# Scores with 64 features: two heads, or two maps, matmul by matmul in turn on the two row halves of TensorE's array

## The chip, the cores and the metric

The kernel runs on one core of one Trainium2 chip. The metric is the device time of one execution in microseconds. Three runs of the kernel before are given, with their median.

## The reference, cut to what matters

Two transformer blocks stand one behind the other, on 512 tokens of 1024 features, in float32. Two of their attention mixers have scores over 64 features, and these are what is changed.

The first block's second mixer is a dilated band attention with 12 heads of 64 features, in three groups of four heads with dilations 1, 4 and 16. Every score gets a bias from a learned table and a band mask; the three groups' outputs are weighted by the softmax of their log-sum-exps:

```python
sc = jnp.einsum('bchnqd,bchnkd->bchnqk', qs, ks).astype(jnp.float32) + bias[:, None]
sc = jnp.where(mask, sc, NEG_INF)
lse = jax.nn.logsumexp(sc, axis=-1)
pr = jnp.exp(sc - lse[..., None]).astype(vs.dtype)
o = jnp.einsum('bchnqk,bchnkd->bchnqd', pr, vs)
...
wts = jax.nn.softmax(jnp.stack(lses, axis=0), axis=0).astype(q.dtype)
o = jnp.sum(wts[..., None] * jnp.stack(outs, axis=0), axis=0)
```

The second block has a causal differential attention with four heads. A head has two maps of 64 features each, and the difference of their softmaxes is applied to the values:

```python
sc = jnp.einsum('bqhmd,bkhmd->bhmqk', q_blk, k).astype(jnp.float32) * scale
sc = sc - slopes[None, :, None, None, None] * dist
sc = jnp.where(dist >= 0, sc, NEG_BIG)
p = jax.nn.softmax(sc, axis=-1)
a = p[:, :, 0] - lam * p[:, :, 1]
```

All other work (projections, gates, three feed-forward nets, the other mixers) is matmuls with 128 rows.

## The kernel before

**Exact products.** Each float32 operand is split into a high part (ScalarE, `.h`) and a low part (VectorE or GpSimd, `.l`), and each product is three fp32r matmuls: high by high, low by high, high by low. Weights come as panels of 512 KB: a load into `raw` (on SyncE's queue, at most three ahead), the high part `wh` on ScalarE (L467), the low part `wl` on VectorE or GpSimd (L469).

**The order of work.** A planner in the kernel writes out every engine's queue by hand before the chip sees it. Projections are "fills": `pump` takes one step of them at a time, three matmuls. All that follows a projection (normalization, scores, softmax, values) is a "job", a generator that yields what it waits for. `flow` runs a job's next step as soon as what it waits for is ready by the planner's own clock, 0.15 us before TensorE's, and otherwise pumps a fill. The planner's costs are formulas. A matmul of n columns is charged n/2400 + 0.0025 us and at least 0.055 us, whichever rows of the array it is on. An add or a maximum of 512 elements on VectorE is charged 0.065 + 0.00105 x 512 = 0.60 us. A transfer is charged 0.5 us at the queue and its bytes at 360 per ns (`dma_fin`). What is once ordered is executed in that order by each engine; the waits on semaphores are worked out from it.

**Banks.** PSUM has eight banks: `FIL` is banks 0 to 3 for projections, `JOB` is banks 4 to 7 for jobs. `bank_of(ring)` waits until a bank of the ring is idle in the planner's state, takes the one that comes free first, and the first matmul into it carries the wait for its last reader (`b.free`).

**Band scores.** Twelve heads are two pairs of heads (`pr` 0 and 1) for each of three groups g (dilations 1, 4, 16). One tile holds the pair's 128 features: head e = 0 on partitions 0 to 63, head e = 1 on partitions 64 to 127. `qb{pr}{g}0` is the pair's queries and `qb{pr}{g}1` its keys. `scores_b(pr)` goes through head 0 and then through head 1; a head has four groups of matmuls, each into a bank of `JOB`: blocks (1, 2) of g = 0, blocks (0, 3) of g = 0, g = 1 and g = 2. These are 6, 6, 12 and 12 matmuls, of 256, 192, 128 and 128 columns. Behind each group VectorE adds the bias (this frees the bank) and takes the maximum, and ScalarE does two or four exponentials. The adds wait for `t_toe`: the bias tables are spread by twelve transfers from `tab_sb` (`relative()`, L169), each with a step of one element.

**Differential scores.** `differential(j)` goes through the query blocks i = 3, 2, 1, 0 of a head. For each it takes a bank for map 0 (partitions 0 to 63), issues its three matmuls of 128(i + 1) columns, then a bank for map 1 (partitions 64 to 127) and its three. `maps` is spawned when both are issued.

The functions that the change touches, and what calls them:

Of the kernel before, what the change touches and what calls it, by code (L numbers as in the profile page):

```python
# [3 lines left out]
S = 512  # L4
# [88 lines left out]
def build(nc, d):  # L93
# [316 lines left out]
    def have(*tiles_):  # L410

        return lambda: all(t.rdy is not None for t in tiles_)
# [546 lines left out]
    def views_b(e):  # L959
        base = p_t[:, 2048 * e:2048 * e + 2048]  # L960
        return (base[:, 0:1024].rearrange("p (b k) -> p b k", b=4),
                [None] + [base[:, 512 + 512 * g:1024 + 512 * g].rearrange("p (c k) -> p c k", c=4) for g in (1, 2)])

    def scores_b(pr, work):
        o_m, o_s, ls_t, f_t = work(24), work(24), work(24), work(24)
        nm, ss, ls, f = (o.rearrange("p (e g b) -> p e g b", e=2, g=3) for o in (o_m, o_s, ls_t, f_t))
        last = []
        for e in range(2):
            hd, hp = 2 * pr + e, slice(64 * e, 64 * e + 64)
            if p_free[e] is None:  # L970
                yield lambda: p_free[e] is not None
            was, p_free[e] = p_free[e], None
            g0, g12 = views_b(e)
            bias0 = bias_t[0][:, hd * 256:hd * 256 + 256]
# [7 lines left out]
            def exps(g, parts):  # L982
                for s, blk, tk in parts:
                    tk = a_act(s, s, FN.Exp, tk, bias=nm[:, e, g, blk:blk + 1], accum_out=ss[:, e, g, blk:blk + 1])
                last.append(tk)

            for g, blks in ((0, (1, 2)), (0, (0, 3)), (1, None), (2, None)):
                if not have(*qk[pr][g])():
                    yield have(*qk[pr][g])
                yield [t.rdy for t in qk[pr][g]]  # L990
                b = yield from bank_of(JOB)
                act_table(EXP)
                if g == 0:
                    for n, blk in enumerate(blks):
                        lo, hi = max(0, 128 * blk - 64), min(S, 128 * blk + 192)
                        scores(b, b.ap[:, 256 * n:256 * n + hi - lo], 0, slice(128 * blk, 128 * blk + 128), slice(lo, hi))
                else:
                    for c in range(4):
                        cs = slice(128 * c, 128 * c + 128)
                        scores(b, b.ap[:, cs], g, cs, cs)  # L1000
                if blks == (1, 2):
                    s = b.ap[:, :].rearrange("p (b k) -> p b k", b=2)
                    t1 = v_tt(g0[:, 1:3, :], s, bias0.unsqueeze(1).to_broadcast([128, 2, 256]), ALU.add, b.done, t_toe, was)
                    b.free = [t1]
                    t2 = v_red(nm[:, e, 0, 1:3], g0[:, 1:3, :], ALU.max, t1, negate=True)
                    exps(0, [(g0[:, 1, :], 1, t2), (g0[:, 2, :], 2, t2)])
                elif blks == (0, 3):
                    p0, p3 = g0[:, 0, 64:256], g0[:, 3, 0:192]
                    t1 = v_tt(p0, b.ap[:, 0:192], bias0[:, 64:256], ALU.add, b.done, t_toe, was)
                    t2 = v_tt(p3, b.ap[:, 256:448], bias0[:, 0:192], ALU.add, b.done, t_toe, was)  # L1010
                    b.free = [t2]
                    t3 = v_red(nm[:, e, 0, 0:1], p0, ALU.max, t1, negate=True)
                    t4 = v_red(nm[:, e, 0, 3:4], p3, ALU.max, t2, negate=True)
                    exps(0, [(p0, 0, t3), (p3, 3, t4)])
                else:
                    bt = bias_t[g][:, hd * 128:hd * 128 + 128]
                    s = b.ap[:, :].rearrange("p (c k) -> p c k", c=4)
                    t1 = v_tt(g12[g], s, bt.unsqueeze(1).to_broadcast([128, 4, 128]), ALU.add, b.done, t_toe, was)
                    b.free = [t1]
                    t2 = v_red(nm[:, e, g, :], g12[g], ALU.max, t1, negate=True)  # L1020
                    exps(g, [(g12[g][:, c, :], c, t2) for c in range(4)])
                yield
        done_b["scores", pr] = now()
        te = last[-1]

# [777 lines left out]
    def differential(j):  # L1803
# [41 lines left out]
        for i in (3, 2, 1, 0):  # L1845
            n, cs = 128 * i + 128, slice(128 * i, 128 * i + 128)
            P = yield from grab(pd, 2)
            bs = []
            for m in range(2):
                hp = slice(64 * m, 64 * m + 64)  # L1850
                b = yield from bank_of(JOB)
# [528 lines left out]
```

How the kernel before makes its waits and increments, by code:

```python
            def go(eng):  # L2315
                for op in queues[ln]:
                    for key, value in op.emit:
                        eng.wait_ge(key.sem, value)
                    ins = op.fn(eng)
                    if isinstance(op.sem, DmaSem):
                        ins.then_inc(op.sem.sem, 16)
                    elif op.used:
                        ins.then_inc(ln.sem, 1)
                if ln is sp:
                    for o in outs:
                        eng.wait_ge(o.sem.sem, o.value)
```

## Time and profile before

| | |
|---|---|
| three runs | 2106.89, 2104.71, 2106.92 us; median 2106.89 us |
| profiled execution, from its first to its last instruction | 2101.4 us |
| median of the runs less that span | 5.5 us |
| the profiled execution's own time | not listed apart from the three runs |
| TensorE busy | 2056.6 us, 98% of the span |
| VectorE, ScalarE, GpSimd busy | 1120.6, 891.7, 333.3 us |
| TensorE's mean granted clock | 0.987 |
| DMA | 191.45 MB, 91 GB/s |

The span is the time between the first and the last instruction of the execution that the profiler recorded. A time of a run holds besides it what lies before and after. In rows of an order of time, the first number is the start in us from the span's start, the second the duration in us; a matmul's duration holds its way through the array, so consecutive ones overlap and the pace is read from the starts. "x2" is two instructions merged into one line. "128*128 128x512" is the stationary operand and then the moving one, partitions by elements; a stationary operand of 64*128 is on one half of the rows. A bracket at the end of a line is the idle time of the engine before it and what ended it.

### The profile page before, as it was taken

To read this page: it belongs to the slowest core of one execution; us is meant where nothing else is said; L and a number is where in the kernel's file an instruction comes from. 1 tells how busy PE (TensorE), PEld (TensorE's weight loads), DVE (VectorE), ACT (ScalarE), POOL (GpSimd) and SP (SyncE) were. 2 spreads that over 40 slices of the span, in tenths; PEclk is the share of its full clock that TensorE was granted. 3 is DMA by queue.
4 is the path that set the end of the run, shared out by engine and by line. 5 is a ranking of instruction groups with operands and counts; after the bars stand their busy time and mean duration, and the time that the engine had idled before them with its cause. 6 is when DMAs were issued, how large, how long until landed. Compare 5 with 4: busy or idle time off the path is not lost.

```text
span 2101.4 us, 25530 instructions
## 1 busy us (share of the span) xinstructions
PE 2056.6 (98%) x9996; PEld 1724.9 (82%) x9996; DVE 1120.6 (53%) x1988; ACT 891.7 (42%) x1755; POOL 333.3 (16%) x320
## 2 busy tenths in 40 slices
PE   8599999999999999999999999999999999999997
PEld 6598888888888888878888888788898888888886
DVE  5346778445544443476443435687775664444434
ACT  4224556234532332464332324677664443322324
POOL 3000533022000000332110101221211011110102
PEclk9699999999999999999999999999999999999999
DMA  7312111224332333233233223223152132332322
GB/s 161 59 51 67 55 51 51 75 86 153 108 100 95 96 100 95 76 110 100 91 100 101 92 89 111 85 66 106 61 175 91 36 105 91 101 100 92 100 90 71
DMA packets 61697, 191.45 MB, mean 91 GB/s; under 512 B 6884, under 2 KB 14564, under 8 KB 61576
## 3 DMA queue, kind: packets, MB, share of 16 engines
q1 hardware_dynamic: 61576, 189.82, 30.0%
q8 instruction: 78, 1.28, 0.3%
q14 instruction: 43, 0.35, 0.1%
HBM read 186.64 MB, written 2.10 MB: 90 GB/s over the span
## 4 chain that ended last, share of the span: by engine, by line
PE 92%; DVE 4%; ACT 1%; SPq 1%; DMA 1%; issue 0%; DVEq 0%; ACTq 0%
PE bank L292 91%; PE bank L297 1%; SPq L169 1%; DVE wl L469 1%; DVE tmp L181 1%; DMA bias<-tab_sb 0%; DVE work L190 0%; ACT wh L467 0%; DVE tmp L184 0%; DMA raw<-d_wts 0%; ACT rsq L178 0%; DVE x_sb L181 0%; DVE work L181 0%; DVE pd L184 0%; DVE pd L196 0%
## 5 line engine op out<-in xcount | busy, mean ns | idle before, releaser
L467 ACT ACTIVATE wh<-raw 128x512 fp32r<-128x512 f32 (+1 forms) x700 | 403.6, 609 | 915.8 <-PE bank L292 912.0
L292 PE MATMUL bank<-h_h,wh 128*128 128x512 f32 x1488 | 591.0, 397 | 7.2 <-ACT wh L467 6.2
L292 PE MATMUL bank<-h_l,wh 128*128 128x512 f32 x1488 | 581.9, 391 | 0.7 <-DVE h_l L184 0.7
L292 PE MATMUL bank<-h_h,wl 128*128 128x512 f32 x1488 | 581.4, 391 | 0.0
L469 DVE TENSOR_TENSOR wl<-raw,wh 128x512 fp32r<-128x512 f32 (+1 forms) x642 | 429.8, 694 | 61.7 <-ACT wh L467 39.8
L292 PEld LDWEIGHTS bank<-h_h,wh 128*128 128x128 f32 x1488 | 280.7, 189 | 68.5 <-ACT wh L467 6.2
L292 PEld LDWEIGHTS bank<-h_l,wh 128*128 128x128 f32 x1488 | 280.8, 189 | 60.6 <-DVE h_l L184 3.0
L292 PEld LDWEIGHTS bank<-h_h,wl 128*128 128x128 f32 x1488 | 280.5, 189 | 59.3 <-DVE wl L469 0.3
L469 POOL TENSOR_TENSOR wl<-raw,wh 128x256 fp32r<-128x256 f32 x114 | 94.6, 858 | 367.2 <-ACT wh L467 367.2
L202 POOL TENSOR_TENSOR tmp<-tmp,rstd 128x512 f32<-128x512 f32 x44 | 63.4, 1442 | 469.4 <-ACT tmp L178 469.4
L181 DVE TENSOR_TENSOR tmp<-bank,rstd 128x512 f32<-128x512 f32 x92 | 64.7, 706 | 116.7 <-PE bank L292 116.1
L181 DVE TENSOR_TENSOR x_sb<-x_sb,bank 128x512 f32<-128x512 f32 x56 | 38.5, 687 | 141.4 <-PE bank L292 141.4
L181 DVE TENSOR_TENSOR tmp<-tmp,bank 128x512 f32<-128x512 f32 x53 | 36.4, 687 | 139.4 <-PE bank L292 133.2
L292 PE MATMUL bank<-f1act_h,wh 128*128 128x512 f32 x256 | 99.6, 389 | 0.0
L292 PE MATMUL bank<-f1act_l,wh 128*128 128x512 f32 x256 | 99.6, 389 | 0.0
L292 PE MATMUL bank<-f1act_h,wl 128*128 128x512 f32 x256 | 99.6, 389 | 0.0
L184 DVE SCALAR_TENSOR_TENSOR x_sb<-bank,x_sb 128x512 f32<-128x512 f32 (+1 forms) x51 | 33.6, 660 | 123.6 <-PE bank L292 123.6
L202 POOL TENSOR_TENSOR ssum<-ssum,tmp 128x512 f32<-128x512 f32 (+1 forms) x52 | 70.6, 1362 | 134.4 <-ACT tmp L178 133.4
L202 POOL TENSOR_TENSOR ssum<-tmp,tmp 128x512 f32<-128x512 f32 (+1 forms) x9 | 12.4, 1385 | 472.2 <-ACT tmp L178 472.2
L292 PE MATMUL bank<-wh,h_h 128*128 128x256 f32 (+1 forms) x264 | 84.0, 318 | 0.0
L292 PE MATMUL bank<-wl,h_h 128*128 128x256 f32 (+1 forms) x264 | 82.4, 312 | 0.0
L292 PE MATMUL bank<-wh,h_l 128*128 128x256 f32 (+1 forms) x264 | 82.2, 311 | 0.0
(473 smaller groups left out, 3513.1 us busy)
## 6 DMA issues: line engine op xcount, KB each, us to landing
raw<-d_wts SPq DMA_DIRECT2D x314, 512.0 KB, 3.5
raw<-d_wts SPq DMA_DIRECT2D x24, 384.0 KB, 3.0
x_sb<-d_xT SPq DMA_DIRECT2D x16, 256.0 KB, 5.4
raw<-d_wts SPq DMA_DIRECT2D x24, 128.0 KB, 2.0
d_yT<-x_sb SPq DMA_DIRECT2D x4, 384.0 KB, 2.9
tab<-d_ali SPq DMA_DIRECT2D x4, 256.0 KB, 4.0
tab<-d_dec SPq DMA_DIRECT2D x4, 256.0 KB, 3.6
mraw<-d_memT SPq DMA_DIRECT2D x8, 128.0 KB, 2.3
```

Of the source, the lines that this page charges most:

```text
L169: op = Op(sp, lambda e: e.dma_start(out, in_), waits, sem)
L181: return dve.add(lambda e: e.tensor_tensor(out, a, b, op), 0.065 + 0.00105 * size(a), waits)
L184: return dve.add(lambda e: e.scalar_tensor_tensor(out, a, s, b, op0, op1, reverse0=rev), 0.1 + 0.00105 * size(a), waits)
L202: return pool.add(lambda e: e.tensor_tensor(out, a, b, op), 0.1 + 0.0022 * size(a), waits)
L292: bank.done = pe.add(lambda e: e.matmul(out, lhsT, rhs, start=first, stop=True, skip_group_check=True), n, w, waits)
L297: bank.done = pe.add(lambda e: e.transpose(out, in_, ident), 0.11, w, waits)
L467: p.th = [Op(act, lambda e, c=c: e.activation(H[:, c], raw[:, c], FN.Copy), [p.load]) for c in (slice(o, min(o + 512, width)) for o in ran ...
L469: p.tl = [Op(low, lambda e, c=c: e.tensor_tensor(L[:, c], raw[:, c], H[:, c].bitcast(F32), ALU.subtract), [p.load, p.th[c.start // 512]]) ...
```

## The change

In the band mixer the loop over the two heads moves inside: `scores_b` waits until both heads' probabilities are free, and then, for each of the four groups, takes two banks and issues the pair's matmuls in turn, one of head 0 and one of head 1, for each of the three products. Then it issues the adds, maxima and exponentials of head 0 and those of head 1. In the differential mixer both banks are taken first, and the three products are issued for map 0 and map 1 in turn. The number of matmuls, adds, maxima and exponentials, their shapes and the planner's costs stay as they are. The middle part of `biased` is as the lines before, with `[e]` added, and is left out here.

```diff
-        for e in range(2):
-            hd, hp = 2 * pr + e, slice(64 * e, 64 * e + 64)
+        heads = slice(0, 64), slice(64, 128)
+        was = []
+        for e in range(2):
             if p_free[e] is None:
                 yield lambda: p_free[e] is not None
-            was, p_free[e] = p_free[e], None
-            g0, g12 = views_b(e)
-            def scores(b, out, g, lq, rk):
-                q, k = qk[pr][g]
-                b_mm(b, out, q.h[hp, lq], k.h[hp, rk], q.rdy[0], k.rdy[0])
-                b_mm(b, out, q.l[hp, lq], k.h[hp, rk], q.rdy[1])
-                q.free = k.free = [b_mm(b, out, q.h[hp, lq], k.l[hp, rk], k.rdy[1])]
+            was.append(p_free[e])
+            p_free[e] = None
+        views = [views_b(e) for e in range(2)]
...
+        def scores(bs, outs, g, lq, rk):
+            q, k = qk[pr][g]
+            for x, y, tq, tk in ((q.h, k.h, q.rdy[0], k.rdy[0]), (q.l, k.h, q.rdy[1], None), (q.h, k.l, None, k.rdy[1])):
+                for b, out, hp in zip(bs, outs, heads):
+                    q.free = k.free = [b_mm(b, out, x[hp, lq], y[hp, rk], tq, tk)]
...
+        def biased(e, b, g, blks):
+            (g0, g12), w = views[e], was[e]
+            if blks == (1, 2):
+                s = b.ap[:, :].rearrange("p (b k) -> p b k", b=2)
+                t1 = v_tt(g0[:, 1:3, :], s, bias0[e].unsqueeze(1).to_broadcast([128, 2, 256]), ALU.add, b.done, t_toe, w)
+                b.free = [t1]
+                t2 = v_red(nm[:, e, 0, 1:3], g0[:, 1:3, :], ALU.max, t1, negate=True)
+                exps(e, 0, [(g0[:, 1, :], 1, t2), (g0[:, 2, :], 2, t2)])
...
+        for g, blks in ((0, (1, 2)), (0, (0, 3)), (1, None), (2, None)):
+            if not have(*qk[pr][g])():
+                yield have(*qk[pr][g])
+            yield [t.rdy for t in qk[pr][g]]
+            bs = []
+            for e in range(2):
+                bs.append((yield from bank_of(JOB)))
+            act_table(EXP)
+            if g == 0:
+                for n, blk in enumerate(blks):
+                    lo, hi = max(0, 128 * blk - 64), min(S, 128 * blk + 192)
+                    outs = [b.ap[:, 256 * n:256 * n + hi - lo] for b in bs]
+                    scores(bs, outs, 0, slice(128 * blk, 128 * blk + 128), slice(lo, hi))
+            else:
+                for c in range(4):
+                    cs = slice(128 * c, 128 * c + 128)
+                    scores(bs, [b.ap[:, cs] for b in bs], g, cs, cs)
+            for e in range(2):
+                biased(e, bs[e], g, blks)
+            yield
@@
             for m in range(2):
-                hp = slice(64 * m, 64 * m + 64)
-                b = yield from bank_of(JOB)
-                out = b.ap[:, 0:n]
-                b_mm(b, out, q.h[hp, cs], k.h[hp, 0:n], q.rdy[0], k.rdy[0])
-                b_mm(b, out, q.l[hp, cs], k.h[hp, 0:n], q.rdy[1])
-                last = b_mm(b, out, q.h[hp, cs], k.l[hp, 0:n], k.rdy[1])
-                bs.append(b)
+                bs.append((yield from bank_of(JOB)))
+            for x, y, tq, tk in ((q.h, k.h, q.rdy[0], k.rdy[0]), (q.l, k.h, q.rdy[1], None), (q.h, k.l, None, k.rdy[1])):
+                for b, hp in zip(bs, (slice(0, 64), slice(64, 128))):
+                    last = b_mm(b, b.ap[:, 0:n], x[hp, cs], y[hp, 0:n], tq, tk)
             spawn(maps(i, P, bs), j)
```

## Rows read from the trace of the kernel before

**Rows 1.** The page: busy time of the engines, and the chain that ended last.

```profile
PE 2056.6 (98%) x9996; PEld 1724.9 (82%) x9996; DVE 1120.6 (53%) x1988; ACT 891.7 (42%) x1755; POOL 333.3 (16%) x320
...
PE 92%; DVE 4%; ACT 1%; SPq 1%; DMA 1%; issue 0%; DVEq 0%; ACTq 0%
```

**Rows 2.** TensorE in order of time, 36 to 61 us: start, duration, instruction.

```profile
39.21 0.27 PE L292 MATMUL bank<-qb001l,qb000h 64*128 64x192 f32 x1
...
42.35 0.41 PE L292 MATMUL bank<-qb011l,qb010h 64*128 64x128 f32 x1
...
43.29 0.63 PE L292 MATMUL bank<-h_l,wh 128*128 128x512 f32 x1
...
47.98 0.63 PE L292 MATMUL bank<-h_h,wh 128*128 128x512 f32 x1
...
49.00 0.40 PE L292 MATMUL bank<-h_h,wh 128*128 128x512 f32 x1
...
52.66 0.39 PE L292 MATMUL bank<-h_l,wh 128*128 128x512 f32 x1
```

**Rows 3.** Windows: PE, PEld, DVE, ACT, POOL busy (xcount), granted clock, DMA share, GB/s.

```profile
42.00:48.00 6.00, 6.00 (x17) 4.72 (x17) 0.00 (x0) 0.00 (x0) 0.00 (x0) 0.50 0.79 27
53.00:60.00 7.00, 7.00 (x32) 6.97 (x30) 0.00 (x0) 0.00 (x0) 0.00 (x0) 1.00 0.65 25
92.00:100.00 8.00, 8.00 (x35) 8.00 (x36) 2.83 (x6) 3.35 (x14) 0.00 (x0) 0.72 0.06 6
```

**Rows 4.** The transfers' queue in order of time, 20 to 100 us.

```profile
29.36 34.76 SPq L169 DMA_DIRECT2D bias<-tab_sb  x12
```

**Rows 5.** VectorE in order of time, 28 to 96 us.

```profile
72.02 0.69 DVE L181 TENSOR_TENSOR pB<-bank,bias 128x512 f32<-128x512 f32 x1 [31.13 <-DMA bias<-tab_sb]
...
73.34 0.61 DVE L181 TENSOR_TENSOR pB<-bank,bias 128x192 f32<-128x192 f32 x2
...
75.71 1.02 DVE L184 SCALAR_TENSOR_TENSOR tmp<-bank,rstd 128x512 f32<-128x512 f32 x1
```

**Rows 6.** TensorE in order of time, 58 to 96 us.

```profile
81.78 0.47 PE L292 MATMUL bank<-qb021h,qb020h 64*128 64x128 f32 x1 [21.61 <-ACT qb021h L178]
...
83.93 0.58 PE L292 MATMUL bank<-qb001h,qb000h 64*128 64x256 f32 x1
...
84.56 0.41 PE L292 MATMUL bank<-qb021l,qb020h 64*128 64x128 f32 x1
...
91.45 0.41 PE L292 MATMUL bank<-qb021l,qb020h 64*128 64x128 f32 x1
91.79 0.60 PE L292 MATMUL bank<-wh,h_h 128*128 128x256 f32 x1
```

**Rows 7.** TensorE in order of time, 183 to 201.5 us.

```profile
183.37 0.32 PE L292 MATMUL bank<-qb111h,qb110h 64*128 64x128 f32 x1
...
184.65 0.27 PE L292 MATMUL bank<-qb111l,qb110h 64*128 64x128 f32 x1
...
195.95 0.32 PE L292 MATMUL bank<-qb121h,qb120h 64*128 64x128 f32 x1
...
200.90 0.27 PE L292 MATMUL bank<-qb121l,qb120h 64*128 64x128 f32 x1
```

**Rows 8.** TensorE in order of time, in three stretches from 1345 to 1439 us.

```profile
1346.16 0.40 PE L292 MATMUL bank<-qk21h,qk20l 64*128 64x512 f32 x2
1346.40 0.40 PE L292 MATMUL bank<-qk21l,qk20h 64*128 64x512 f32 x2
...
1372.41 0.27 PE L292 MATMUL bank<-std0h,dvl 128*128 128x128 f32 x1
...
1373.67 0.40 PE L292 MATMUL bank<-h_l,wh 128*128 128x512 f32 x1
...
1437.47 0.40 PE L292 MATMUL bank<-h_h,wl 128*128 128x512 f32 x1
...
1438.61 0.39 PE L292 MATMUL bank<-h_l,wh 128*128 128x512 f32 x1
```

More of the change, by code:

```diff
@@ L967, in scores_b @@
         last = []
+        heads = slice(0, 64), slice(64, 128)
+        was = []
         for e in range(2):
-            hd, hp = 2 * pr + e, slice(64 * e, 64 * e + 64)
             if p_free[e] is None:
                 yield lambda: p_free[e] is not None
-            was, p_free[e] = p_free[e], None
-            g0, g12 = views_b(e)
-            bias0 = bias_t[0][:, hd * 256:hd * 256 + 256]
-            def scores(b, out, g, lq, rk):
-                q, k = qk[pr][g]
-                b_mm(b, out, q.h[hp, lq], k.h[hp, rk], q.rdy[0], k.rdy[0])
-                b_mm(b, out, q.l[hp, lq], k.h[hp, rk], q.rdy[1])
-                q.free = k.free = [b_mm(b, out, q.h[hp, lq], k.l[hp, rk], k.rdy[1])]
@@ L982, in exps @@
[L982 to L990, printed above, removed]
-                b = yield from bank_of(JOB)
[L992 to L1022, printed above, removed]
@@ new lines, in scores_b @@
+            was.append(p_free[e])
+            p_free[e] = None
+        views = [views_b(e) for e in range(2)]
+        bias0 = [bias_t[0][:, hd * 256:hd * 256 + 256] for hd in (2 * pr, 2 * pr + 1)]
+        def scores(bs, outs, g, lq, rk):
[3 more added lines that the diff above has]
+                    q.free = k.free = [b_mm(b, out, x[hp, lq], y[hp, rk], tq, tk)]
@@ new lines, in exps @@
+        def exps(e, g, parts):
+            for s, blk, tk in parts:
+                tk = a_act(s, s, FN.Exp, tk, bias=nm[:, e, g, blk:blk + 1], accum_out=ss[:, e, g, blk:blk + 1])
+            last.append(tk)
+        def biased(e, b, g, blks):
[6 more added lines that the diff above has]
+                exps(e, 0, [(g0[:, 1, :], 1, t2), (g0[:, 2, :], 2, t2)])
+            elif blks == (0, 3):
+                p0, p3 = g0[:, 0, 64:256], g0[:, 3, 0:192]
+                t1 = v_tt(p0, b.ap[:, 0:192], bias0[e][:, 64:256], ALU.add, b.done, t_toe, w)
+                t2 = v_tt(p3, b.ap[:, 256:448], bias0[e][:, 0:192], ALU.add, b.done, t_toe, w)
+                b.free = [t2]
+                t3 = v_red(nm[:, e, 0, 0:1], p0, ALU.max, t1, negate=True)
+                t4 = v_red(nm[:, e, 0, 3:4], p3, ALU.max, t2, negate=True)
+                exps(e, 0, [(p0, 0, t3), (p3, 3, t4)])
+            else:
+                bt = bias_t[g][:, (2 * pr + e) * 128:(2 * pr + e) * 128 + 128]
+                s = b.ap[:, :].rearrange("p (c k) -> p c k", c=4)
+                t1 = v_tt(g12[g], s, bt.unsqueeze(1).to_broadcast([128, 4, 128]), ALU.add, b.done, t_toe, w)
+                b.free = [t1]
+                t2 = v_red(nm[:, e, g, :], g12[g], ALU.max, t1, negate=True)
+                exps(e, g, [(g12[g][:, c, :], c, t2) for c in range(4)])
@@ new lines, in scores_b @@
+        for g, blks in ((0, (1, 2)), (0, (0, 3)), (1, None), (2, None)):
[11 more added lines that the diff above has]
+                    scores(bs, outs, 0, slice(128 * blk, 128 * blk + 128), slice(lo, hi))
+            else:
+                for c in range(4):
[4 more added lines that the diff above has]
+            yield
@@ L1849, in differential @@
             for m in range(2):
-                hp = slice(64 * m, 64 * m + 64)
-                b = yield from bank_of(JOB)
-                out = b.ap[:, 0:n]
-                b_mm(b, out, q.h[hp, cs], k.h[hp, 0:n], q.rdy[0], k.rdy[0])
-                b_mm(b, out, q.l[hp, cs], k.h[hp, 0:n], q.rdy[1])
-                last = b_mm(b, out, q.h[hp, cs], k.l[hp, 0:n], k.rdy[1])
-                bs.append(b)
+                bs.append((yield from bank_of(JOB)))
+            for x, y, tq, tk in ((q.h, k.h, q.rdy[0], k.rdy[0]), (q.l, k.h, q.rdy[1], None), (q.h, k.l, None, k.rdy[1])):
+                for b, hp in zip(bs, (slice(0, 64), slice(64, 128))):
+                    last = b_mm(b, b.ap[:, 0:n], x[hp, cs], y[hp, 0:n], tq, tk)
             spawn(maps(i, P, bs), j)
```

## The prediction

> **What bounds the kernel now.** I read the page first, to see which engine is busy and which engine the chain of waits follows, then the order of time on TensorE around every matmul of the edited scores, then the queue that ends TensorE's one long idle time. The page shows TensorE busy for 98% of the span, and the chain lies on it for 92% [rows 1]. A microsecond taken from TensorE's work is therefore a microsecond of the total, wherever TensorE is the chain. The exception is early. TensorE runs out of work at 60.2 us and sits idle for 21.61 us [rows 2, 6]. The cause is not a matmul. The twelve transfers that spread the bias table are issued one after another from 29.36 us for 34.76 us [rows 4], and VectorE's first add of a bias starts only at 72.02 us [rows 5]. All that stands behind that add on VectorE, and behind the exponentials on ScalarE, waits with it, qb021h too, for which TensorE waits. So before 72 us TensorE's work costs nothing as long as there is any it may do, and what counts is how much work is left for after 72 us.
>
> **How the row halves run today.** In the restart after the stall the second head's first matmul starts at 83.93 us, while the first head, which stands wholly ahead of it in the program, starts its last one at 84.56 us [rows 6]. The second half of the array runs ahead of the program's order by three or four matmuls. Hence a map with three matmuls is overtaken whole: in the differential stage the two maps' matmuls start together, "x2" in one line, and the next two start 0.24 us later, a single matmul's spacing [rows 8]. There the change has little left to give. In the band stage a head has 36 matmuls, so nearly all of them run alone, and there the gain lies.
>
> The Trainium skill says otherwise (TensorE: Matmul & The Clock Gate, Part 3, "What overlaps and what doesn't"): matmuls start and end strictly in the program's order. The start at 83.93 us ahead of one issued earlier goes against it. What its rule would give is a rival below.
>
> **Step 1, band pair 1 (169 to 201 us).** The first head's group for dilation 4 stands alone: 12 matmuls from 183.37 to 184.65 us, 1.28 us. The last stretch has the first head's last 12 and the second head's 36, from 195.95 to 200.90 us, 4.95 us [rows 7]. After the change the second head's matmuls go beside the first's in the three places where those stand now, so the last stretch also becomes 12 steps: 4.95 - 1.28 = 3.67 us saved. Nothing else is on the chain there (TensorE is busy without a gap), so all of it counts. Does the pace hold with both halves at work? In the overlap of rows 6 each half keeps its spacing, and the 512-column pair of rows 8 goes at 0.24 us. So I take full overlap. The bounds are nothing saved and 3.67 us.
>
> **Step 2, differential maps.** Of the 16 pairs of maps 14 start together now. Two, one of 384 columns and one of 128, are apart by some microseconds, because the second map's bank came later. The lone second map costs, between its neighbours and less their own spacing of 0.11 and 0.23 us, 1373.67 - 1372.41 - 0.34 = 0.92 us, and 1438.61 - 1437.47 - 0.46 = 0.68 us [rows 8]. The change joins them when both banks are there. The softmax of a block is started after both maps already, so nothing comes later. Saved: 1.6 us, with 0 as the lower bound.
>
> **Step 3, band pair 0: the banks.** This works against the change. The ring JOB has four banks. Today the first head's first three groups take three idle ones and the fourth is left for dilation 16, so TensorE is through its scores at 42.6 us and can run projections until 60.2 us, all before the bias is there. After the change each group takes two banks: blocks (1, 2) take two, blocks (0, 3) the other two. The group of dilation 4 then needs banks that only the adds give back, and these can't start before 72.02 us. Will the planner put fills ahead of it? Its own costs say few. It charges 0.60 us for an add and 0.60 us for a maximum, so it sees the second bank free some 2 us after the first pair of groups, of which the second pair covers 1 us, and one step of a projection is 0.65 us: two steps, six matmuls, instead of the single step that stands behind blocks (0, 3) now. It counts 0.5 us for each bias transfer, and so doesn't know of the 42 us.
>
> Blocks (0, 3) are through at about 39.3 us [rows 2], as now, since both halves work at once, and six wide matmuls take 1.4 us. TensorE thus stops at about 41 us instead of 60.2 us. When it goes on: the first matmul needs the first add (72.02 us), the second the second head's, which stands behind one maximum as the next add does now, at 73.34 us, and takes 0.69 us like the first [rows 5]; with a hand-over this is 74.1 us. Then come 12 steps at the low clock, at (91.45 - 83.93)/35 = 0.215 us each, and 0.34 us to the first wide matmul [rows 6]: 76.8 us. Then the work that was done before the stall: 30 matmuls of 512 columns (the 33 between 42.7 and 52.9 us less the three moved ahead) and 30 of 256 columns with strided weights, 7.1 us up to 60.0 us [rows 2, 3].
>
> For the clock: the granted clock was 0.50 from 42 to 48 us, and 0.72 from 92 to 100 us, which is 4.5 us at the low of the two levels (1.2 GHz) and the rest at 2.4 GHz [rows 3]. After the start of full-height work it stayed low until about 48.4 us in the one case (5.7 us) and 96.5 us in the other (4.7 us). I take 5.2 us: 12 matmuls at (47.98 - 43.29)/11 = 0.426 us; the other 18 take (52.66 - 49.00)/16 = 0.229 us each, 4.1 us in all [rows 2]. So 76.8 + 5.1 + 4.1 + 7.1 = 93.1 us. Last the pair for dilation 16: 1.28 us and four breaks of 0.1 us (as 91.45 to 91.79 us is 0.1 longer than a step), 1.7 us: 94.8 us. The fill that starts at 91.79 us now starts 3.0 us later. Bounds: if the clock stays low for all 30, 18 x 0.197 = 3.5 us more; if the planner puts all the projections ahead, a gain of 3.0 us (first rival). The strided matmuls don't change with the clock: 7.0 us holds 32 matmuls, all but one or two of them strided, at a clock of 1.00, and 8.0 us holds 35 at 0.72 [rows 3]. They add nothing.
>
> The Trainium skill warns that row tiling puts more pressure on PSUM (TensorEngine Tiling (Array Packing), Gotcha 1). It gives no price; the one here is from the rows above.
>
> **Costed at nothing.** The number of matmuls, adds and exponentials is the same. The second head's eight exponentials for its first three groups move ahead of the projections' splits on ScalarE, and its adds ahead of those on VectorE, in both pairs. For pair 0 the splits on ScalarE fall into TensorE's idle time now, and the panels are first needed at 91.79 us [rows 6]. Pair 1 now has to wait for both heads' probabilities to be free; the values of pair 0 end before it starts anyway.
>
> **Sum.** +3.0 - 3.67 - 1.6 = -2.3 us on a span of 2101.4 us. The listed times don't say which execution was profiled; the median is 5.5 us above the span, which I take for what lies around it. 2106.9 - 2.3 = 2104.6 us, a tenth of a per cent, less than the 0.2% (4.2 us) that a measurement of this kernel can tell.
>
> **Rivals.** *The banks don't stop TensorE* (chance 0.15). If the planner runs the projections first, or the banks come otherwise, the stall ends by its present chain, later only by the second head's adds and maxima, as long as the first's, 75.71 - 72.02 = 3.7 us [rows 5]. Then 12 steps take the place of what lies between 81.78 and 91.79 us: 85.5 + 0.27 + 2.4 + 0.34 = 88.5 us, 3.3 us sooner. Sum -3.3 - 3.67 - 1.6 = -8.6 us: 2098.3 us. Against it is the count of banks.
>
> *The halves in turn gain nothing* (0.10). If alternating the halves at every matmul cost what the overlap saves, the moved stall remains: +3.0 us, 2109.9 us. For it: rows 6 show only three or four overlapped steps at a stretch. Against it: the maps of rows 8.
>
> *Slower: the weights come late* (0.15). ScalarE does sixteen exponentials where it now does eight before it splits the next weights. Now those splits fall into TensorE's idle time. Should a panel used right after the restart have its split behind the exponentials, TensorE waits again, from about 77 us, until those of dilation 4 (done some 5 us after the scores) and a split with its subtraction (about 2 us) are through: 7 us more, 2104.6 + 7 = 2111.6 us. It decides from 6.5 us on. Against it: the fills up to 60 us found all their weights while ScalarE was already stuck.
>
> *Strict order* (0.04). If the page's rule held and the "x2" were an artefact of the records, the maps would run one after another today and the change would halve them. That would save 3 x (0.23 + 0.18 + 0.12 + 0.11) = 1.9 us for each of four heads, 7.7 us in place of the 1.6: 2098.5 us (0.23 and 0.11 are the spacings of rows 8 and 7, the two between are by columns). Against it: the six matmuls of rows 8 do fit between their neighbours only if they overlap.
>
> **How the numbers follow.** My forecast holds 0.50, the rest (0.06) is a plan that shifts elsewhere. Its own range is 2101 to 2108.5 us: the clock's bound above, and about 3.5 us of a shifted plan below. The range over the cases is 2098 to 2111 us. Faster by over 0.2%, below 2102.7 us: 0.15 + 0.04 + 0.07 of the forecast and 0.03 of the rest, 0.29. Slower, above 2111.1 us: 0.15 with 0.02 of the no-gain case and 0.03 of the rest, 0.20. Within: 0.51.
>
> **What would show it.** In the profile after: TensorE's idle of some 30 us begins near 41 us, in front of a matmul of qb011h, released by VectorE's add into pB; projections run from 77 to 93 us; the score matmuls stand as "x2" at 0.11 us near 170, 183 and 196 us, 12 steps each; all 16 pairs of maps are joined. I am wrong if TensorE still idles from 60 us, or if the matmuls of a pair stand one behind the other.

## The result and the profile after

The changed kernel took 2115.07 us (median of 4, 2113.63 to 2116.29) where the kernel before, on the same chip, took 2106.02 us (4). The ratio is 1.0045, 95% interval [1.0031, 1.0059]: slower by 9 us, outside the predicted range and of the other sign than its middle. The profiled span is 2112.9 us against 2101.4 us. A time is longer than its span by 1.7 to 2.2 us in every execution on record, not by the 5.5 us that the prediction took; so the profiled execution of the kernel before took some 2103.2 us. The 63 other executions of it whose span is on record have 2101.4 to 2105.4 us: the profile is one of the quickest.

The page of the changed kernel (busy time of the engines, then the chain) answers to [rows 1]. TensorE's busy time fell by 9.4 us, and its share of the span fell as well:

```profile
PE 2047.2 (97%) x9996; PEld 1715.1 (81%) x9996; DVE 1124.0 (53%) x1985; ACT 891.1 (42%) x1755; POOL 347.1 (16%) x325
...
PE 92%; DVE 4%; ACT 2%; SPq 1%; DMA 1%; issue 1%; POOL 0%; DVEq 0%; ACTq 0%; POOLq 0%
```

TensorE in order of time in the changed kernel, around the stall; this answers to [rows 2, 6]. The step at 40.28 us is the last before the wait:

```profile
40.28 0.40 PE L292 MATMUL bank<-h_h,wl 128*128 128x512 f32 x1
72.71 0.47 PE L292 MATMUL bank<-qb011h,qb010h 64*128 64x128 f32 x1 [32.03 <-DVE pB L181]
74.03 0.47 PE L292 MATMUL bank<-qb011h,qb010h 64*128 64x128 f32 x1 [0.85 <-DVE pB L181]
...
76.23 0.62 PE L292 MATMUL bank<-qb011l,qb010h 64*128 64x128 f32 x2
76.78 0.79 PE L292 MATMUL bank<-h_h,wh 128*128 128x512 f32 x1
...
79.47 0.40 PE L292 MATMUL bank<-h_h,wh 128*128 128x512 f32 x1
...
94.59 0.28 PE L292 MATMUL bank<-qb021l,qb020h 64*128 64x128 f32 x2
94.79 0.51 PE L292 MATMUL bank<-wh,h_h 128*128 128x256 f32 x1
```

The last of these is the first panel matmul behind pair 0's scores. Before, that place is at 91.79 us [rows 6], 3.00 us earlier. The same view at pair 1's last group: twelve steps of both heads, where one head's 12 and the other's 36 matmuls followed each other [rows 7].

```profile
197.69 0.33 PE L292 MATMUL bank<-qb121h,qb120h 64*128 64x128 f32 x2
...
198.97 0.28 PE L292 MATMUL bank<-qb121l,qb120h 64*128 64x128 f32 x2
```

So the edit did on the spot what it was to do. The loss is elsewhere, and the waits of TensorE between 205 and 435 us (engine, line, tile waited for: us in total, times, longest) show the first part of it:

```profile
PE bank L292 <- ACT pa L178: 3.6, 2, 2.7
PE bank L292 <- DVE outa_l L181: 0.8, 1, 0.8
PE bank L292 <- DVE work L181: 0.6, 1, 0.6
PE bank L292 <- DVE pta_l L181: 0.4, 1, 0.4
```

The kernel before had one wait of 0.6 us in that view, for pa. The second part shows after 1484 us. Windows of the changed kernel (busy us and count of PE, PEld, DVE, ACT, POOL, then granted clock, DMA share, GB/s):

```profile
1494.00:1524.00 30.00, 28.04 (x159) 24.07 (x158) 26.75 (x46) 19.96 (x42) 12.66 (x12) 1.00 0.10 32
1524.00:1558.00 34.00, 30.92 (x222) 28.98 (x221) 23.96 (x44) 21.74 (x47) 9.07 (x9) 0.95 0.54 171
```

and of the kernel before:

```profile
1494.00:1524.00 30.00, 29.07 (x185) 25.82 (x183) 24.37 (x41) 18.93 (x42) 11.36 (x10) 1.00 0.20 65
1524.00:1558.00 34.00, 33.57 (x266) 32.82 (x265) 28.21 (x55) 25.25 (x57) 5.62 (x7) 1.00 0.61 187
```

Idle time in the 64 us rose from 1.36 to 5.04 us. The granted clock was at its low level (0.50) for 3.4 us from 1554 us, right behind the longest wait (2.2 us); the mean of 0.95 over 34 us is 1.7 us of lost time.

For a ledger I number the matmuls with wh or wl (the panels) in order of time; every kernel has the same ones (the two padded ones add none with a panel), so the n-th of them, counted from 0, marks the same progress of the projections. The table gives its start in each kernel less its start before, in us. A profile's first matmuls already differ by up to 1.4 us, so one row means little below that; changes along a row count.

| n-th panel matmul (start before) | 400 (139) | 600 (192) | 640 (205) | 860 (274) | 1300 (429) | 5400 (1347) | 5900 (1484) | 6300 (1555) |
|---|---|---|---|---|---|---|---|---|
| the change | +1.71 | +1.75 | -1.91 | +4.65 | +4.18 | +4.18 | +1.23 | +11.53 |
| band | +2.55 | +2.59 | -1.07 | +4.84 | +3.31 | +3.32 | +3.35 | +3.64 |
| diff | +0.30 | +0.30 | +1.88 | +1.85 | +1.89 | +1.89 | -1.12 | +6.92 |
| band1 | -0.31 | -0.25 | -3.91 | +3.15 | +2.05 | +2.08 | +2.09 | +2.15 |
| noturn | +5.41 | +6.75 | +4.05 | +8.15 | +13.16 | +13.16 | +12.10 | +14.45 |
| unturn | +4.32 | +5.66 | +2.96 | +9.33 | +7.84 | +7.89 | +4.93 | +12.96 |
| cal | +0.51 | +0.51 | +2.09 | +14.11 | +6.92 | +6.94 | +10.43 | +22.29 |
| tick | +0.36 | +0.38 | +3.54 | +13.15 | +9.77 | +9.81 | +10.92 | +11.18 |
| frozen | +0.63 | +0.63 | +2.21 | +2.19 | +2.11 | +2.14 | +2.09 | +2.11 |
| fix0 | -6.73 | -6.67 | -10.33 | -4.43 | -5.89 | -5.87 | -5.91 | -5.88 |
| p0fixf | -6.57 | -6.57 | -3.45 | -3.50 | -3.57 | -3.53 | -3.58 | -3.55 |
| pinned | +2.64 | +2.67 | -0.98 | -0.72 | -0.76 | -0.72 | -0.76 | -0.74 |
| rejoin | -5.79 | -5.74 | -9.39 | -9.13 | -9.18 | -9.16 | -9.15 | -9.14 |

In the changed kernel pair 1 gives 3.66 us (192 to 205 us), the first attention part takes 6.1 (to 429 us), and nothing moves for 900 us. Then the row falls by 2.95 us and rises by 10.3. Those two belong together, since a mark counts panels alone: of TensorE's other matmuls, 244 stand between the marks of 1347 and 1484 us and 68 between those of 1484 and 1555 us before, and 226 and 86 in the changed kernel. Eighteen have moved behind the middle mark, and with them some 4.8 us of work. Only the sum counts, 7.36 us from 1347 to 1555 us.

Between marks with equal numbers of all matmuls (x1194, x1214) a loss can be split. The changed kernel, marks 640 to 1300 and 5400 to 6300, then the kernel before:

```profile
203.26:432.80 229.54, 224.02 (x1194) 187.79 (x1193) 155.03 (x312) 113.02 (x243) 66.11 (x69) 0.99 0.19 57
1351.44:1566.98 215.54, 208.49 (x1214) 175.24 (x1213) 167.40 (x355) 150.15 (x327) 62.74 (x64) 0.99 0.29 91
```

```profile
205.17:428.62 223.45, 222.59 (x1194) 186.55 (x1193) 153.00 (x310) 112.81 (x243) 66.76 (x73) 1.00 0.19 59
1347.26:1555.45 208.19, 206.61 (x1214) 174.34 (x1213) 167.17 (x362) 150.36 (x327) 50.03 (x55) 1.00 0.30 94
```

In the first stretch TensorE's idle time rises by 4.7 us, and 3.4 us at the low clock cost 1.7, together 6.4 us. In the second it is 5.5 and again 1.7 us, together 7.2. The losses are 6.1 and 7.36 us, so TensorE's own work changed by -0.3 and +0.2 us.

### The profile page after: what moved, and what is told of

Same layout as the page of the kernel before. It is cut to its first block, busy times and chain, and to the rows that moved or that the text cites. A ratio compares the mean times of both kernels' runs of the same rounds, so it can differ in the third digit from the quotient of the medians.

```text
span 2112.9 us, 25514 instructions
## 1 busy us (share of the span) xinstructions
PE 2047.2 (97%) x9996; PEld 1715.1 (81%) x9996; DVE 1124.0 (53%) x1985; ACT 891.1 (42%) x1755; POOL 347.1 (16%) x325
## 4 chain that ended last, share of the span: by engine, by line
PE 92%; DVE 4%; ACT 2%; SPq 1%; DMA 1%; issue 1%; POOL 0%; DVEq 0%; ACTq 0%; POOLq 0%
PE bank L292 90%; PE bank L297 1%; SPq L169 1%; DVE wl L469 1%; DMA bias<-tab_sb 0%; DVE tmp L181 0%; ACT wh L467 0%; ACT rsq L178 0%; DVE work L190 0%; DVE tmp L184 0%; DMA raw<-d_wts 0%; DVE x_sb L181 0%; DVE work L181 0%; DVE rsq L184 0%; POOL ssum L202 0%
```

## Experiments: which part loses it

Times below are medians, with the ratio to the kernel before that ran beside it. **band** has only the band part of the change, **diff** only the differential part, **band1** only pair 1 of the band part:

```
-        for e in range(2):                 # band1: pair 0 keeps this
+        if pr in (1,): both heads a group  # and pair 1 takes the new text
```

> Only the band part of the change; the differential maps as before. The changed kernel lost time in two places: +4.2 us over before by 430 us (+1.75 pair 0, -3.66 pair 1, +6.1 in the attention with 128 features behind it), and +7.3 us more between 1345 and 1560 us. Theory 'two separate parts': the band part carries the first, the differential part the second, so this kernel is 4.2 us above before and its trace runs level with before from 430 us on. Rival 'one shift disturbs all later plans': a later stage moves too, and the total is 4.2 us plus or minus several us.

> Only the differential part. Theory 'two separate parts': level with before up to 1345 us, then +7.3 us. My prediction's own step 2 says -1.6 us. Rival 'the planner's order of the band part causes it': -1.6 us or nothing here.

> Both heads in turn only in pair 1 of the band mixer; pair 0 and the differential maps as before. Pair 0's stall must be the old one (21.6 us before 81.8 us) and pair 1 must save 3.7 us. If the attention behind it loses its 6 us through pair 1, the total is +2.4 us; if it loses them through pair 0's order, the total is -3.7 us.

Band took 2109.76 us, 1.0017 [1.0007, 1.0026]; diff 2111.5 us, 1.0028 [1.0017, 1.0039]; band1 2105.38 us, 0.9998 [0.9989, 1.0008]. The table places them. Band and band1 both gain 3.66 us at pair 1 and both then lose 4.4 and 6.0 us in the first attention part; diff loses 5.0 us between 1347 and 1555 us, and 1.6 us at 192 to 205 us by a low clock that is told further down. The 4.4 and 6.0 us are one loss: the waits are the same to 0.1 us, and band1, like the changed kernel, has 1.7 us of low clock behind the longest of them, band none. The parts are separable, and each loses in a stretch in which its own matmuls no longer run.

**pad** asks whether TensorE, early by the gain, merely waits there. It repeats the last group of pair 1 three times, 36 steps or 4.0 us, unseen by the planner:

```
+                if (pr, g) == (1, 2):
+                    t, fin = pe.t, [b.done.fin for b in bs]
+                    for again in range(3): ...      # the group's scores again
+                    pe.t = t                        # nothing booked
```

> The changed kernel with the last group of pair 1 of the band mixer computed four times over (72 extra matmuls, 36 steps of 0.11 us, 4.0 us on TensorE), not charged by the planner, so that every queue keeps its order; the result is unchanged. Theory 'TensorE got ahead of VectorE and ScalarE': the time saved in pair 1 is given back in waits further on, so adding it again costs nothing, 0 to 0.5 us over the changed kernel. Rival 'the order of the new plan costs it, wherever TensorE stands': the full 4.0 us are added.

It took 2118.39 us, 1.0062 [1.0046, 1.0079], 3.3 us above the changed kernel. In the trace its panels stand 1.7 us behind that kernel's ahead of the pad, 5.8 at 205 us, 4.1 at 429 us and 3.4 at 1555 us: of the 4.0 us some 2.3 vanish, of which 1.7 in the first attention part (by the medians 0.7). These 1.7 us are not TensorE waiting less. Its waits in this part are those of the changed kernel one by one (the longest 2.70 us in both, idle time 5.50 and 5.52 us), though it comes 5.8 us later; what is missing is the changed kernel's low clock behind that longest wait (0.74 and 0.92 in its two windows of 5 us from 275 us, 1.00 in pad throughout). So no part of the loss is TensorE being early: 4.7 of the 6.1 us are idle time that stays wherever TensorE stands, and 1.7 a low clock that comes with that wait in one profile and not in the next. **pad2** does the same to the diff kernel with ten repeats of the last pair of maps (30 steps, 3.3 us, near 1440 us):

> The kernel with the differential part of the change alone, and at the last pair of maps the six score matmuls issued ten more times (60 matmuls of 128 columns, some 30 steps of 0.11 us, 3.3 us of TensorE work that changes only what is overwritten), which the planner does not see, so that the order on every other engine stays. Rival (TensorE arrives early in the memory stage and waits there for VectorE): the 3.3 us vanish in its waits and this takes 0 to 1 us more than the kernel with the differential part alone, at 2111.5 to 2112.5. Theory (the planned order alone costs it, TensorE is nowhere ahead): 3.3 us more, at 2114.5 to 2115. A value between divides the loss between the two.

It took 2115.15 us, 1.0044 [1.003, 1.0058]; in the trace it stays 3.5 us behind diff from there to the end. Nothing is absorbed, so in the memory stage, too, TensorE was not ahead of anything.

## Experiments: turns, grouping, or the plan

**noturn** has the change's groups and banks, planned with the matmuls head by head:

```
-                for b, out, hp in zip(bs, outs, heads):   # inner loop
+            for b, out, hp in zip(bs, outs, heads):       # outer loop
```

> The changed kernel with its grouping kept (both heads of a pair in one group, both banks taken first; both maps of a row chunk likewise), but the matmuls issued head by head and map by map, not in turn on the row halves. Theory (the loss is the order of the work elsewhere that comes with the grouping): the in-turn issue is worth its local gain of some 5 us and nothing of the loss, so that this comes out 3 to 8 us above the changed kernel, at 2118 to 2123, with the first attention part again losing some 4 to 6 us between 205 and 430 us and the memory stage 5 to 7. Rival (taking turns itself fills the banks faster than their readers empty them, and that is the loss): the two losses go away with the turns, and this comes out at 2103 to 2108. In the band groups the bare matmul starts with both row halves in one step go to the number of before.

It took 2115.14 us, 1.0043 [1.0028, 1.0059], the same as the changed kernel: the theory's 3 to 8 us more did not come. The table says why it settles nothing: it loses 9.1 us in the first attention part and 1.3 in the last stage, the change 6.1 and 7.35. The two plans differ, so their totals can't be compared. From here on I compare turns in one and the same plan. **unturn** lets the planner write the changed kernel, and only then sorts TensorE's list:

```
+            ops = pe.items[-6:]                   # band: the last 12 or 24
+            pe.items[-6:] = ops[0::2] + ops[1::2]
```

> The changed kernel, planned exactly as it was; only afterwards the matmuls of each group of scores are put back head by head and map by map in TensorE's list, so that it has the changed kernel's order on every other engine and none of its turns. It measures what the turns are worth in one and the same plan. Theory (turns gain what the steps say, 12 steps instead of 24 in a group of 24): 5 to 10 us more than the changed kernel, 2120 to 2125. Rival (what they gain is lost again in waits for banks): within 2 us of the changed kernel, as the kernel planned without turns was.

It took 2116.09 us, 1.0053 [1.0039, 1.0067], only 1.0 us above the changed kernel (2.1 us when each is taken against the kernel before beside it), which is what the rival said. In the trace it stands 4.9 us behind the changed kernel at 205 us and 3.7 at 429 us, and makes up 2.3 us after 1534 us, of which 1.7 are the low clock that the changed kernel has there (its window above) and this one doesn't. Over both stretches unturn has some 1.6 us less idle time (4.1 and 4.4 us above before, the changed kernel 4.7 and 5.5), so the rival's reason holds for that part, and the clock is the other. Nor was a group back at 24 steps. TensorE in order of time in unturn:

```profile
202.55 0.27 PE L292 MATMUL bank<-qb121l,qb120h 64*128 64x128 f32 x1
202.56 0.38 PE L292 MATMUL bank<-qb121h,qb120h 64*128 64x128 f32 x2
202.72 0.33 PE L292 MATMUL bank<-qb121h,qb120l 64*128 64x128 f32 x2
202.83 0.32 PE L292 MATMUL bank<-qb121l,qb120h 64*128 64x128 f32 x2
202.94 0.27 PE L292 MATMUL bank<-qb121h,qb120h 64*128 64x128 f32 x1
```

The second head overlaps the first for its last matmuls, as in [rows 6], and a group of 24 takes 21 steps. From 139 to 205 us, where neither has idle time or a low clock, the changed kernel gains 3.6 us and unturn 1.4: of pair 1's gain 2.3 us are the turns and 1.4 the grouping by itself.

**frozen** is the kernel before, with 14 pairs of maps put in turn in TensorE's list after planning:

```
+            if pe.items[-6:] == six:
+                pe.items[-6:] = [six[n] for n in (0, 3, 1, 4, 2, 5)]
```

> The kernel before, planned exactly as before; only afterwards, where the six score matmuls of a pair of maps lie next to each other in TensorE's list (14 of the 16 pairs), they are put in turn there. Every other engine's list stays as it was. Theory (the differential part lost its time by the new plan, its turns gain): 1.5 to 3 us less than the kernel before, at 2102.5 to 2104.5, with no loss after 1484 us. Rival (taking turns itself makes the readers of the banks late in this stage): the loss of 5 us after 1484 us stays, at 2108 to 2111.

It took 2105.42 us, 1.0001 [0.9993, 1.001], and its row is flat to 0.05 us from 1347 to 1555 us. Turns neither cost nor gain anything there; the theory's gain was wrong, the prediction's view of these 14 pairs right. A small pair before, in order of time, and then the same pair in frozen:

```profile
1358.84 0.33 PE L292 MATMUL bank<-qk21h,qk20h 64*128 64x128 f32 x2
1359.00 0.28 PE L292 MATMUL bank<-qk21h,qk20l 64*128 64x128 f32 x2
1359.11 0.28 PE L292 MATMUL bank<-qk21l,qk20h 64*128 64x128 f32 x2
```

```profile
1360.98 0.33 PE L292 MATMUL bank<-qk21h,qk20h 64*128 64x128 f32 x2
1361.14 0.27 PE L292 MATMUL bank<-qk21h,qk20l 64*128 64x128 f32 x2
1361.25 0.28 PE L292 MATMUL bank<-qk21l,qk20h 64*128 64x128 f32 x2
```

Then two runs that change no matmul and no group, only what the planner books. From that it chooses the order and also which of VectorE and GpSimd takes a subtraction (GpSimd has 320 instructions before, 325 in the changed kernel, 346 in tick), so "order" here means both. **cal** books what the trace shows for a small matmul, **tick** 10 ns more for a transpose:

```
-        n = max(n, 0.055) if lhsT.dtype == F32R else max(4 * n, 0.108)
+        n = max(n, 0.111 if size(lhsT) == 128 else 0.06) if lhsT.dtype == F32R else max(4 * n, 0.108)
```

```
-        bank.done = pe.add(lambda e: e.transpose(out, in_, ident), 0.11, w, waits)
+        bank.done = pe.add(lambda e: e.transpose(out, in_, ident), 0.12, w, waits)
```

> The kernel before, with one figure of its planner changed: the least time that it books for a matmul of 4-byte rounded operands, 0.111 us with 128 weight columns and 0.06 us below that, as the trace shows, where it booked 0.055. No matmul, bank or group is changed; only the order that the plan writes out may differ. Theory (the order of the plan alone moves the time by as much as the changed kernel lost): a time that differs from the kernel before by 2 to 10 us in either direction. Rival (the plan's order is worth nothing by itself and the loss needs the change's own grouping): within 2 us of the kernel before.

> The kernel before, with the time that its planner books for a transpose 0.12 us instead of 0.11, and nothing else: a second change of the plan alone, smaller than the one of the charge for small matmuls. Theory (any new plan draws its own losses, some 2 to 15 us, since the one at hand leaves TensorE hardly idle): slower than the kernel before by 2 to 15 us, the loss between 205 and 430 us and after 1485 us, where the orders differ. Rival (that other figure was a bad one in itself): within 2 us of the kernel before.

Cal took 2125.58 us, 1.0094 [1.008, 1.0107], with the truer figure. Tick took 2114.42 us, 1.004 [1.0026, 1.0054]. A new order alone costs 20 us in cal and 9.5 us in tick, most of it in the same two stretches (in tick nearly all in the first, with another 3.2 us at 192 to 205 us). The waits of TensorE in tick, 205 to 430 us:

```profile
PE bank L292 <- DVE pta_l L181: 2.2, 3, 1.3
PE bank L297 <- ACT pa L178: 1.8, 1, 1.8
PE bank L292 <- DVE outa_l L181: 0.9, 1, 0.9
```

## Experiments: the change with the old order behind it

**pinned** is the change with the planner led back. It books 0.7 us more on ScalarE after each of pair 1's groups, which is enough for VectorE's, ScalarE's, GpSimd's and the transfers' lists to be those of the kernel before from about 227 us on, and puts the 14 pairs of maps in turn afterwards:

```
             for e in range(2):
                 biased(e, bs[e], g, blks)
+            if pr == 1:
+                act.t += 0.7
             yield
```

> The change, with the planner brought back to the order of the kernel before behind it: the band part as it is (no hold), 0.7 us booked on ScalarE after each of pair 1's groups, and 14 of the 16 pairs of maps put in turn in TensorE's list alone. From the end of pair 1's scores on the lists of all engines but TensorE's are those of the kernel before. Theory (the change's own terms are a small gain, and all of its loss is the order elsewhere): +1.7 us of pair 0 and -3.7 of pair 1, or -5.2 where the kernel before runs pair 1 at a lower clock, and 0 for the maps: 2101.5 to 2104.5 us, faster than the kernel before by 0.05 to 0.2%. Rival (part of the 10 us is the change's own doing): 2107 us or more.

It took 2102.57 us, 0.9989 [0.998, 0.9998], just clear of noise: 2.3 us below the kernel before, where the change itself is 9.0 us above. The row is flat from 274 us to the end. The windows of 1347 to 1557 us, pinned first, then the changed kernel, show the idle time go from 7.05 back to 1.59 us (before: 1.58):

```profile
1347.00:1557.00 210.00, 208.41 (x1232) 176.18 (x1231) 170.04 (x365) 151.32 (x329) 50.57 (x55) 1.00 0.31 96
```

```profile
1347.00:1557.00 210.00, 202.95 (x1159) 168.52 (x1158) 162.13 (x345) 145.81 (x315) 61.67 (x63) 0.99 0.29 91
```

Pinned leaves the two pairs of maps that lie apart as they were, so what joining those two is worth with the old order was not measured.

**fix0** goes at pair 0's moved stall: the band part, with the dilation-4 group held back until the dilation-16 tiles are there, so that the projections come ahead of the wait.

```
+            if (pr, g) == (0, 1):
+                if not have(*qk[0][2])():
+                    yield have(*qk[0][2])
+                yield [t.rdy for t in qk[0][2]]
```

> The band part of the change alone, with the first pair's dilation-4 group held until the dilation-16 tiles are there, so that the wait for the bias transfers begins behind the projections that were left for after it: TensorE is to stand still from about 60 us and not from 40. Theory (pair 0's wait is only moved work: what TensorE does before the wait is taken off behind it): 6 to 8 us less than the kernel with the band part alone, seen as about -6 us between 100 and 190 us where that kernel shows some +2; the time comes out at 2101 to 2104 if the first attention part's loss of 4 to 5 us stays. Rival (the projections already stand in the wait or later work is bound by VectorE): within 1 us of the band part alone, near 2109.5.

**p0fixf** is that hold with pair 0 alone in turn, pair 1 as before, and the maps as in frozen; **rejoin** is fix0 with the 0.7 us of pinned.

> Pair 0 in turn, with its dilation-4 group held until the dilation-16 tiles are there; pair 1 as in the kernel before; the maps in turn in the list only, as in the run that keeps the plan. The order on the other engines differs from before in pair 0's own stretch alone. Theory (what stays local stays gained): the -6.7 us of pair 0 and the -1.5 to -3 us of the maps add up, with no loss between 205 and 430 us and none after 1484 us: 2095.5 to 2098 us, 1 to 3 us below the held pair 0 with all of the band part in turn. Rival (the gain ahead of 205 us is lost in the first attention part whatever the plan, as some 4 us were in the other runs): 2100 to 2102.

> The held pair 0 with the whole band part in turn, and one figure for the planner: after each of pair 1's four groups it books 0.7 us more on ScalarE, with which its list on every engine runs from the end of pair 1's scores on as in the kernel before (that kernel had lost 4.4 us between 205 and 430 us). Theory (the first attention part lost its time by the order that came with pair 1's grouping, and by nothing that the grouping itself does): those 4.4 us come back, 2093.5 to 2095.5, with the difference to the kernel before flat from 215 us to the end. Rival (TensorE arriving some 10 us early has to wait there in any order, or 1.6 to 3 us are lost to a low clock as in the run with pair 1 head by head): 2097 to 2099.

Fix0 took 2098.69 us, 0.9966 [0.9953, 0.9978]; its row runs 9.3 us below band's. TensorE's order of time in fix0:

```profile
54.13 0.39 PE L292 MATMUL bank<-wl,h_h 128*128 128x256 f32 x1
72.68 0.47 PE L292 MATMUL bank<-qb011h,qb010h 64*128 64x128 f32 x1 [18.15 <-DVE pB L181]
...
84.62 0.41 PE L292 MATMUL bank<-qb021l,qb020h 64*128 64x128 f32 x2
84.96 0.60 PE L292 MATMUL bank<-wh,h_h 128*128 128x256 f32 x1
```

Its first panel after the stall starts at 84.96 us, against 91.79 us before [rows 6]. Rejoin took 2093.53 us, 0.9946 [0.9934, 0.9959], the fastest of all, flat from 274 us: the 4.4 us that band and fix0 lost in the first attention part are gone, though TensorE gets there over 9 us early. Its waits up to 420 us, from 195 us on:

```profile
PE bank L297 <- DVE pa L187: 0.6, 1, 0.6
PE bank L292 <- DVE work L181: 0.3, 1, 0.3
```

P0fixf took 2099.8 us, 0.9972 [0.9961, 0.9984], 2 us above the expected range and close to its rival's. Its order stays old as meant and nothing is lost after 205 us, but 3.1 us go between 192 and 205 us. The windows name it; p0fixf and then the kernel before:

```profile
190.00:195.00 5.00, 5.00 (x45) 5.00 (x44) 3.96 (x9) 2.58 (x13) 0.00 (x0) 0.88 0.35 105
195.00:200.00 5.00, 5.00 (x15) 4.01 (x15) 2.89 (x5) 4.63 (x22) 0.00 (x0) 0.50 0.00 0
200.00:205.00 5.00, 5.00 (x42) 5.00 (x41) 3.78 (x8) 1.88 (x5) 0.00 (x0) 0.94 0.37 105
```

```profile
195.00:200.00 5.00, 5.00 (x44) 4.57 (x43) 3.23 (x6) 1.01 (x5) 0.00 (x0) 1.00 0.29 108
200.00:205.00 5.00, 5.00 (x35) 4.56 (x35) 4.48 (x10) 4.83 (x25) 0.00 (x0) 1.00 0.00 0
```

At the end of the 48 half-height matmuls (189.4 to 194.8 us) the granted clock falls to the low level. Of the seven kernels with pair 1 head by head, six show this in their profile (diff, pad2, cal, frozen, tick, p0fixf), at 1.6 to 3.2 us in the table or its trace; only the profile of before does not. Of the nine with pair 1 grouped none does. So the profile on which the prediction rests was a quick execution of its kernel, as its span says too. That fits the medians: pinned is 2.3 us below before, while its profile is 0.7 us below. The length of the run alone does not do it, as far as one profile can tell: pad has 48 half-height steps in a row at the same place, 5.3 us, but with both halves at work, and stays at the high level:

```profile
199.40:204.80 5.40, 5.40 (x97) 5.36 (x96) 0.00 (x0) 0.00 (x0) 0.00 (x0) 1.00 0.32 97
```

## Why the prediction was wrong

**What bounds the kernel: right.** TensorE's busy time counts where it is not idle. But that was taken to mean that the rest of the kernel stays as it is.

**The halves today: right.** A half running ahead is in every trace; the strict order that the Trainium skill states (TensorE: Matmul & The Clock Gate, Part 3) would have given frozen some 6.8 us (the prediction's 7.7 less the two pairs that frozen leaves), and it gained none.

**Step 1: right.** -3.67 predicted, -3.66 in the changed kernel, band, band1 and fix0. Against the usual execution, at a low clock behind the single matmuls, it is some 1.6 us more.

**Step 2: right for the 14 pairs.** They gave nothing by themselves. The two apart were joined, but the 1.6 us can't be seen: the 2.95 us ahead at 1484 us are work that had moved behind that mark, and from 1347 to 1555 us TensorE's time less idle and low clock is 206.6 us before, 206.8 in the changed kernel and 206.9 in diff. The order had changed too, so what the joining alone gives stays open.

**Step 3: right in its mechanism; its exact number is partly luck.** The stall moved to where the banks said, the panel at 94.79 us was forecast at 94.8. The two errors in it cancel. The clock came back 2.7 us after the restart (76.78 to 79.47 us), not 5.2, which saves 1.1 us over the wide matmuls; and 66 panel matmuls stand before the last group, not 60. The 2.7 us are chance: in the three other kernels with this stall and this order behind it the clock came back after 3.0 us (band), 4.4 (pinned) and 4.7 (pad). The six more are not lost, they are missing later: at 139 us 1.71 us are left of the 3.0.

**Costed at nothing: the step that failed.** It weighed only what the second head's adds and exponentials delay next door. The kernel's lists are written by a planner that orders all later work by booked times, and the change moves those times at pair 1 and at the maps. It put nothing down for that. With the new order 6.1 us were lost in the first attention part and 7.36 from 1347 to 1555 us. Pinned shows it for the total: with the old order behind it the change gives 2102.57 us, and neither loss occurs; cal and tick show that such a loss needs no change in TensorE's work. That pinned gains the forecast's 2.3 us is luck: against the usual execution it is some +2.6 for pair 0, -5.2 for pair 1 (the low clock included) and +0.3 behind it, where the forecast had +3.0, -3.67 and -1.6. The prediction had named the case, "a plan that shifts elsewhere", and given it 0.06, though each edit of a group was bound to cause a new plan. The trace names both losses in full, as idle time (4.7 and 5.5 us) and low clock behind the longest wait (1.7 and 1.7 us). Why the planner's order makes TensorE wait at each place was not followed. That TensorE comes early plays no part: pad's waits are the same 5.8 us later, and rejoin, which is earlier still, has hardly any.

**The rivals.** *The banks don't stop TensorE* was refuted as a forecast; fix0 realised it, with -6.7 us at 192 us where -3.3 was worked out. *The halves in turn gain nothing* is refuted: in one and the same plan they gain 2.3 us at pair 1 (unturn). *The weights come late* did not occur: the panels ran from 76.78 us without a wait. *Strict order* is refuted.

## What to carry over

In a kernel whose instruction lists come from a planner, an edit has two effects: its own, and a new order for everything behind it. The second can be far the larger (here +11 us against -2), and no new plan here bettered the old one by chance. All eight kernels with a new plan lost time behind the edit, though these are only four different orders in each of the two stretches: the changed kernel, band, band1 and fix0 have one and the same in the first, the changed kernel and diff in the second. So give it a term ahead of the local sum, and measure the edit with the plan held: sort the finished list, or book a few tenths of a microsecond until the later lists are the old ones. And when an edit takes more banks at once in front of a long wait, hold it back until all work that could be done before the wait is issued. When two kernels are laid side by side by marks, count all work between the marks: where some has moved across one, a gain on one side and a loss on the other are the same thing.

## What was unexpected of the hardware

At the end of a run of 48 half-height matmuls of one half after the other (5 us, no idle time) the granted clock fell to 0.50, for 6.8 us in p0fixf and tick and for 3.4 us in diff, pad2, cal and frozen. Behind the groups of 24, in turn or head by head, it never did, nor in pad's 48 steps with both halves at work, which is one profile.

After the long stall and the half-height steps behind it the clock was back 2.6 to 5.9 us after full-height work began, over all sixteen profiles. That alone moves a profile by more than a microsecond, so a ledger from single profiles can't tell such differences apart.
